# Where the one-column products stand: modulation sums out of three down projections, into a norm's wait and the local attention; position statistics in four pieces

## The reference, cut to what matters

```
m = silu(c) @ ada_w[layer] + ada_b[layer]            # 1024 x 6144 per layer
sh1, sc1, g1, sh2, sc2, g2 = split(m, 6)
h = rms_norm(x, norm_mix_g) * (1 + sc1) + sh1
x = x + g1 * mixer(h)                                # layer 0: LRU and stick breaking; layer 1: local attention
h = rms_norm(x, norm_ffn_g) * (1 + sc2) + sh2
x = x + g2 * ffn(h)                                  # gate and up 1024 x 2816, down 2816 x 1024
```

## Time and profile before

| | us |
|---|---|
| time, median of 3 (lowest, highest) | 2935.57 (2933.58, 2941.92) |
| span of the profiled execution | 2940.3 |
| PE busy, matmuls | 2841.3 (97%) |
| PE weight loads | 2319.8 (79%) |
| DVE, ACT, POOL busy | 1744.2, 1222.0, 1077.7 |
| one-column products of the modulation in the stages and the stick attention (L1243) | 80, as 160 matmuls |
| one-column products of the statistics (L1088) | 16, as 32 matmuls |

### The profile page before, as it was taken

One profiled execution on the slowest core, in us unless ns is written; L12 is line 12 of the kernel. 1 busy time (PEld: TensorE's weight loads), 2 busy tenths in 40 slices (PEclk: granted clock), 3 DMA queues, 4 the chain that ended last, 5 costly groups with the idle time before them and its releaser, 6 DMA issues.

```text
span 2940.3 us, 38997 instructions
## 1 busy us (share of the span) xinstructions
PE 2841.3 (97%) x13385; PEld 2319.8 (79%) x13396; DVE 1744.2 (59%) x2106; ACT 1222.0 (42%) x2059; POOL 1077.7 (37%) x490
## 2 busy tenths in 40 slices
PE   6999999999899999999889999999999999999999
PEld 5767788887677888888658888888888889888887
DVE  7486776776556554668666334557666766544333
ACT  3574432223554322244453222256556665522221
POOL 1312344443213444444314444444422442244443
PEclk9999999999999999999989999999999999999999
DMA  6255263643112333332003333333201330133332
GB/s 217 86 173 185 84 204 98 207 134 91 36 36 79 93 100 93 93 95 87 29 15 93 93 94 98 95 88 94 87 30 52 88 93 30 51 93 93 99 95 93
DMA packets 366012, 278.96 MB, mean 95 GB/s; under 512 B 13490, under 2 KB 321075, under 8 KB 365875
## 3 DMA queue, kind: packets, MB, share of 16 engines
q1 hardware_dynamic: 364624, 276.83, 31.1%
q10 hardware_dynamic: 1251, 0.33, 0.0%
HBM read 275.03 MB, written 2.10 MB: 94 GB/s over the span
## 4 chain that ended last, share of the span: by engine, by line
PE 67%; DVE 3%; ACT 2%; issue 2%; POOL 0%; DVEq 0%; ACTq 0%; POOLq 0%
PE banks L1158 13%; PE banks L1153 12%; PE banks L1162 12%; PE banks L1022 6%; PE banks L1028 6%; PE banks L1025 6%; PE banks L1427 2%; PE banks L995 1%; PE banks L1367 1%; PE banks L1493 1%; PE banks L1155 1%; PE banks L1356 0%; PE banks L1063 0%; PE banks L1400 0%; PE banks L1401 0%
## 5 line engine op out<-in xcount | busy, mean ns | idle before, releaser
L873 POOL TENSOR_TENSOR w_lo<-w_raw,w_hi 128x1024 fp32r<-128x1024 f32 (+1 forms) x423 | 1027.1, 2428 | 1706.8 <-ACT w_hi L1641 1705.8
L1641 ACT ACTIVATE w_hi<-w_raw 128x1024 fp32r<-128x1024 f32 (+1 forms) x424 | 445.6, 1051 | 1131.3 <-PE banks L1162 799.4
L1022 PE MATMUL banks<-w_hi,h_hi 128*128 128x512 f32 x960 | 387.1, 403 | 1.4 <-ACT h_hi L1822 1.4
L1028 PE MATMUL banks<-w_lo,h_hi 128*128 128x512 f32 x960 | 377.3, 393 | 0.7 <-POOL w_lo L873 0.7
L1025 PE MATMUL banks<-w_hi,h_lo 128*128 128x512 f32 x960 | 376.6, 392 | 0.7 <-DVE h_lo L596 0.7
L1153 PE MATMUL banks<-h_hi,w_hi 128*128 128x512 f32 x1280 | 339.0, 393 | 6.7 <-ACT h_hi L1822 6.7
L1158 PE MATMUL banks<-h_lo,w_hi 128*128 128x512 f32 x1280 | 320.8, 391 | 2.5 <-DVE h_lo L596 2.4
L1153 PEld LDWEIGHTS banks<-h_hi,w_hi 128*128 128x128 f32 x1280 | 240.9, 188 | 63.9 <-issue 8.4
L1158 PEld LDWEIGHTS banks<-h_lo,w_hi 128*128 128x128 f32 x1280 | 240.3, 188 | 57.5 <-DVE h_lo L596 8.3
L1162 PE MATMUL banks<-h_hi,w_lo 128*128 128x512 f32 x1152 | 284.5, 389 | 0.0
L1162 PEld LDWEIGHTS banks<-h_hi,w_lo 128*128 128x128 f32 x1152 | 216.2, 188 | 44.9
(11 more groups left out here) (364 smaller groups left out, 4260.6 us busy)
## 6 DMA issues: line engine op xcount, KB each, us to landing
Z<-in_ada_w SPq DMA_DIRECT2D x64, 512.0 KB, 5.0
w_raw<-in_m_w_up SPq DMA_DIRECT2D x64, 512.0 KB, 3.9
w_raw<-in_m_w_down SPq DMA_DIRECT2D x64, 512.0 KB, 3.7
w_raw<-in_kv_w SPq DMA_DIRECT2D x48, 512.0 KB, 3.7
w_raw<-in_ffn_w_gate SPq DMA_DIRECT2D x44, 512.0 KB, 3.7
w_raw<-in_ffn_w_up SPq DMA_DIRECT2D x44, 512.0 KB, 3.7
tmp<-in_ada_w SPq DMA_DIRECT2D x32, 512.0 KB, 4.6
w_raw<-in_ffn_w_down SPq DMA_DIRECT2D x32, 512.0 KB, 3.9
```

The source lines that it names most:

```text
L873: pool.tensor_tensor(wlo[j][:, 0:n], raw[j][:, 0:n], whi[j][:, 0:n], ALU.subtract).then_inc(s_wlo, 1)
L1022: pe.matmul(t, hh, wh, start=k == 0, stop=False)
L1028: mm = pe.matmul(t, hh, wl, start=False, stop=k == DC - 1)
L1641: act.activation(whi[par][:, 0:kc * P], raw[par][:, 0:kc * P], ACT.Copy).then_inc(s_whi, 1)
```

## The change

It has four parts.

1. Block 5 leaves the units of the output projection of layer 0. Its 8 products stand in the wait of the norm that follows, each with one unread matmul behind it, in place of the 12 unread ones. DVE's `modulation` of that block moves from the front of the norm behind the first FFN stage.
2. The second down projection keeps block 7 alone (1 product behind a unit), the third has none and becomes a loop on PE. The loads of `ada_w` and DVE's additions stay where they were.
3. Blocks 8 to 11 have their products in the local attention, 8 in a row ahead of the scores of heads 2, 5, 8 and 11. Their sums and results lie in other tiles and in bank 4, and their `modulation` (blocks 8 to 11, and one norm factor) is DVE's last work ahead of the barrier behind the attention.
4. The 8 products of `token_stats` stand in pairs behind each position block of the panel's second unit. ACT's part follows after its third unit, DVE's after the tables.

```
-        steps[-1][1].products, steps[-1][1].ada = (0, [3]), (0, 8, 8)
-        steps.append(("mods", 1))
+        steps[-1][1].ada = (0, 8, 8)
         ffn(0)
+        steps.insert(next(n for n, (k, st) in enumerate(steps) if k == "gemm" and st.kind == "ffn") + 1, ("mods", 1))
         downs = [st for k, st in steps if k == "gemm" and st.kind == "down" and st.rhs == "mid"]
-        for st, blocks, ada in zip(downs, ([0], [1, 2], [3, 4, 5]), ((8, 16, 8), (24, 16, 8), (40, 8, 4))):
-            st.products, st.ada = (1, blocks), ada
+        for st, blocks, ada in zip(downs, ([0], [1], None), ((8, 16, 8), (24, 16, 8), (40, 8, 4))):
+            st.products, st.ada = blocks and (1, blocks), ada
...
-        steps += [("bar", None), ("window", None), ("bar", None)]
+        steps += [("bar", None), ("window", None), ("mods", 3), ("bar", None)]
...
-            t, o = (bank[6], 2 * P) if FIRST * DC <= c < 5 * DC else (bank[7], 0)
+            t, o = (bank[6], 2 * P) if FIRST * DC <= c < 6 * DC else (bank[7], 0) if c < 8 * DC else (bank[4], 0)
...
+                        if l == 1 and st.norm.raw and st.norm.fresh and st is first_of(st.norm):
+                            token_stats(st.norm, b)
...
-                    if l == 0 and st.norm.raw and st.norm.fresh and st is first_of(st.norm):
-                        token_stats(st.norm)
...
-            def token_stats(norm):
+            def token_stats(norm, b):
                 pe.wait_ge(n_add, past((DC + 1) * norm.sum_index))
-                for k in range(2 * NB):
+                for k in range(2 * b, 2 * b + 2):
...
-                    keep_rate(12)
+                    if si == 2:
+                        for t in range(DC):
+                            products(0, [3], t, 1)
+                            keep_rate(1)
+                    else:
+                        keep_rate(12)
...
                     pe.wait_ge(e["probs"], past(h - 2))
+                    if h % 3 == 2 and h < 12:
+                        products(1, [2 + h // 3])
...
-                    if l == 0 and st.norm.raw and st.norm.fresh and st is first_of(st.norm):
+                    if l == 2 and st.norm.raw and st.norm.fresh and st is first_of(st.norm):
...
+                elif part == 2:
+                    modulation(6, 8, [(1, 0)])
                 else:
-                    modulation(6, 12, [(1, 0), (1, 1)])
+                    modulation(8, 12, [(1, 1)])
...
+                if st.normed:
+                    head_tables(st)
                 if st.norm.raw and st.norm.fresh and st is first_of(st.norm):
                     token_stats(st.norm)
                 if st.normed:
-                    head_tables(st)
```

More of the change, by code:

```diff
@@ L539, in program @@
         ada_parts = [dict(blocks=range(FIRST, 6), sums=[zt(2 * b, 2) for b in range(4)], ring=[TMP[:, 2 * j * S:(2 * j + 2) * S] for j in range(4)], before=0),
-                     dict(blocks=range(6, 12), sums=[zt(16 + 2 * b, 2) for b in range(6)], ring=[zt(28 + 2 * j, 2) for j in range(4)], before=32)]
+                     dict(blocks=range(6, 12), sums=[zt(16 + 2 * ((b + 4) % 6), 2) for b in range(6)], ring=[zt(28 + 2 * j, 2) for j in range(4)], before=32)]
         def ada_source(block, k, n=1):
@@ L557, in ada_add @@
             q = ada_parts[part]
-            t = q["sums"][b] if isinstance(b, int) else zt(2 * b, 2)
+            t = q["sums"][b]
             i = DC * b + k
@@ L1081, in dil_turn @@
                 mm.then_inc(dl["max_turned"], 1)
-            def token_stats(norm):
+            def token_stats(norm, b):
                 pe.wait_ge(n_add, past((DC + 1) * norm.sum_index))
-                for k in range(2 * NB):
+                for k in range(2 * b, 2 * b + 2):
                     block = sq_sum[:, k * P:(k + 1) * P] if k < NB else by_class(sq_sum)[:, k - NB, :]
                     mm = pe.matmul(bank[7][:, k:k + 1], block, ones[:, 0:1], start=True, stop=True)
-                mm.then_inc(n_ss, 1)
+                if b == NB - 1:
+                    mm.then_inc(n_ss, 1)
             def post(st, l, par, u, half):
```

## The result

| | before | changed |
|---|---|---|
| time, median of 12 (lowest, highest), us | 2940.51 (2933.58, 2944.69) | 2947.09 (2935.90, 2954.02) |
| ratio of the times, 95% interval | | 1.0025 [1.0017, 1.0034] |
| span of the profiled execution, us | 2940.3 | 2952.2 |

What follows compares the result with a forecast made beforehand. PE was taken as the bound at most places, DVE in the third down projection, ACT in a norm. Gains of 8.45 us less costs of 6.5 gave 1.9 off the median 2935.6: 2933.7 us, range 2929 to 2939.

Steps and rivals of the forecast that it cites:

- the class of no measurable change: Whole kernel: the result stays within about 0.3%, 8.8 us, of the time before; chance 0.89.
- the attention's term in the sum: Local attention: four rows of 8 products cost 6.1 us, 0.4 at head 2 and 5.7 at heads 5, 8, 11.
- rival 1: Local attention: the rows of products lower the clock, 1.7 us a fall; two give 2937.1, four 2940.5; chance 0.15.
- Output projection, -1.85: Layer 0's output projection: 1.7 us gained from products leaving units, 0.15 from a bias addition leaving the norm's front.
- Norm's wait, 0: Norm after the output projection: eight products with unread matmuls end 0.2 us before h_hi, cost 0, bounds 0 and 0.5.
- Second down, -2.1: Second down projection: 8 products of 0.26 us leave PE's path, gain 2.1 us.
- Third down, -1.4: Third down projection: 24 products go, only two units' 0.72 us each count, gain 1.4 us, bounds 0.7 and 5.0.
- Attention, +6.1 and 0.4: Local attention: rows of products cost 6.1 us, DVE's later work ahead of the barrier behind it 0.4 us.
- Statistics, -3.1: Position statistics in two panels: pairs of products avoid the clock falls, gaining 1.6 us each, 3.1 together.
- rival 2: Position statistics: the clock fall stays despite pairs, the gain of 3.4 us goes, 2937.1; chance 0.12.
- Rival 3: Output and second down projections: DVE becomes the bound in place of the products, 3.8 us of gain go, 2937.5; chance 0.06.
- Rival 4: Third down projection: DVE's chain shortens too, up to 3.6 us more gain, 2930.1; chance 0.07.

Runs made afterwards that it cites:

- the kernel with 4 of the 32 products: Changed kernel with only the last product of each block in the local attention, 4 in place of 32: 2935.58 us, 0.9984 of the kernel before.
- parts 1 and 4 alone: Two kernels, each the kernel before with one part of the change: part 1, ratio 0.9999; part 4, 1.0006, in a second series 0.9998.
- The four kernels of the first series: Kernel before with only some parts of the change, on one chip: 2 and 3, 1.0044; 1, 0.9999; 4, 1.0006; 1 and 4 together, 1.0001.
- parts 2 and 3: Kernel before with parts 2 and 3 of the change alone: 2951.15 us against 2936.86, ratio 1.0044.
- products back: Changed kernel with blocks 8 to 10 behind the third down projection's units, block 11 alone in the attention at head 2: 2933.14 us, 0.9982 of before.
- part 4 again: Kernel before with part 4 of the change alone, run a second time on another chip: 2937.26 us against 2937.93, ratio 0.9998.

## Why the prediction was wrong

The time, 2947.09, lies outside the range (up to 2939), though the class of no measurable change holds. Part of the distance is no matter of the change: the forecast started from the median of three executions, 2935.57, and the kernel before itself has 2940.51 by twelve, which is 4.9 of the 13.4 us between forecast and result. The other 8.5 are the change: -1.9 forecast, +6.6 measured.

The step that failed is the attention's term in the sum, 6.1 us for the rows with nothing for the clock, and with it the argument against rival 1: "the stick attention's rows stand in just such a stream at 1.00". It was one execution of a thing that differs between executions: in two of eighteen profiles the clock falls behind the stick attention's row too. In its place the runs show 6.04 us of own time and about 5 us of clock loss besides (changed against the kernel with 4 of the 32 products, error 2.0). The shape of the failure was named and a fall priced right (1.7 us, as measured), with 2940.5 for four, and given 0.15.

- *Output projection, -1.85*: right, -1.87 and -1.84. *Norm's wait, 0*: right, with room: a product with its unread matmul takes 0.35 us, not 0.48, and all are through 1.0 us before h_hi.
- *Second down, -2.1*: right, -2.05.
- *Third down, -1.4*: the size of the work was right, its effect not. The stage takes 42.8 us on average in the six profiles with 24 products there; in eight with none and a fall in the stage it takes 43.1, so 41.4 without the fall's 1.7: 1.4 less, and the two profiles with none and no fall have 41.1 and 41.4. DVE gets through its last two additions about when it did before (its next operation starts at 672.04, before at 672.69), so the PE that is ahead only waits longer: 1.8 to 3.0 us in the nine profiles without products or unread matmuls there, at most 1.44 in the six. In 8 of the nine the clock falls behind that wait, in none of the six. What is saved goes to the clock.
- *Attention, +6.1 and 0.4*: right as far as own time goes: +6.04 with both. Heads 5, 8 and 11 cost 1.8 each, head 2 with the work of DVE 0.6; the barrier's wait grew from 1.50 to 1.81. Wrong in that the clock was left out: four profiles hold 10 falls, which is 4.25 us a profile, and the clock loss says 5.
- *Statistics, -3.1*: about -1.50 and -0.66 in every profile with part 4. Both falls stand in all three profiles without part 4 and in none of the fifteen with it, so rival 2 is out. The rule of the Trainium skill that stood for it ("TensorE: Matmul & The Clock Gate", section "Why this matters for your kernels": avoid idle gaps of PE between bursts) does not account for these two falls: they came and went with a row of products, without an idle gap. The second gives less because 0.86 us of POOL's low weights come to light; most likely PE, held up by the fall, had been late enough to hide them.
- *Rival 3*: in the second down projection it didn't happen; in the third it is what DVE does. *Rival 4*: no.

Summed over the stages, the attention at its time without falls, the change is 0.0 us (-1.84 - 2.05 + 0 + 6.04 - 2.16), not -1.9: the third down projection and the second statistics make the difference. Of the rest up to +6.3, 4 to 5 come from the rows in the attention, through the clock. Some 1 to 2 us stay open, no more than the error. What parts 1 and 4 alone should give (stages -1.84 and -2.16) doesn't show: +0.1 for part 1, +0.1 for part 4 by both series. The four kernels of the first series all stand 2 to 5 us above the sum of their stages (for parts 2 and 3 with 4 to 5 us of clock added), while those with 4 products, with products back and with part 4 again stand 0.4 to 1.2 above. The kernel before ran 2 to 3 us faster on that chip than on the others, so part of the gap may lie there; no run settles it. The differential attention, which no part touches, loses 5 to 12 us to the clock from one profile to another (3 to 7 falls); whether what is saved ahead makes such falls more likely, these runs can't tell.

## What to carry to other kernels

A short row of one-column products costs PE its own time and may cost nearly as much again through the clock, likely above all right behind a wait; put such products singly behind long matmuls, in a norm's wait, or two by two. Before you call a place safe because the clock stood at 1.00 there, look at it in several executions, and price the falls into the likely case, not into a rival. The median of three executions was 4.9 us below that of twelve here, more than the change that was forecast: start from more. Work that is taken off PE just ahead of a point where it waits for another engine buys a longer wait, and the wait may lower the clock.

## What was unexpected of the hardware

- The loss of clock differs between executions of one kernel, and that makes most of their spread: the changed kernel's 12 ran at a mean clock of 0.987 (2954.02 us) to 0.993 (2935.90), 18 us apart.
- At the position statistics a fall stands in every profile with 8 products in a row and in none with pairs between matmuls of 512 columns (3 of 3, 0 of 15, twice each), while 8 in a row in the attention or the stick attention lower the clock in some executions only.
- DVE's addition of 128 x 1024 takes 1.27 to 1.28 us, and 2.68 (changed) or 2.86 (before) where POOL's split of weights runs beside it.
- A one-column product between matmuls of 512 columns takes 0.24 to 0.26 us behind fp32 matmuls, but only 0.14 (307.05 to 307.19, from its start to the next matmul's) behind an unread bf16 one.
- 32 matmuls of 256 columns, one behind each product, lengthened the attention by 1.0 us in all, 0.03 each.
